# Attention passes of the hybrid block: two branches of a head run as one step instead of one pass per step

## The reference, cut to what matters

```python
s = einsum("bqgrd,bqgkd->bqgrk", q, k) * scale + bias      # selected keys, then once more for the window
p = masked_softmax(s, dist >= 0)
o = einsum("bqgrk,bqgkd->bqgrd", p, v)
o = g[:, :, 0] * o_cmp + g[:, :, 1] * o_slc + g[:, :, 2] * o_win
y = sigmoid(g_conv) * conv_module(...) + sigmoid(g_attn) * nsa_attention(...)
```

## Time and profile before

| | |
|---|---|
| median of 3 runs | 1822.02 us (1819.73 to 1822.78) |
| profiled execution | 1821.97 us, span of its core 1820.2 us |
| PE busy | 1733.0 us, 95% of the span |
| DVE busy | 1250.7 us, 69% |
| ACT busy | 877.8 us, 48% |
| mean granted clock of PE | 0.995 |

### The profile page before, as it was taken

The page is one execution under the profiler, slowest core; times in us unless marked ns, Lnnn a source line. Parts: engine busy times, 40 slices in busy tenths (PEclk is TensorE's granted clock), DMA queues, the critical chain, the costliest instruction groups (busy, mean ns, idle before and its releaser), DMA issues.

```text
span 1820.2 us, 33142 instructions
## 1 busy us (share of the span) xinstructions
PE 1733.0 (95%) x12198; PEld 1588.6 (87%) x12198; DVE 1250.7 (69%) x2120; ACT 877.8 (48%) x1411; POOL 74.3 (4%) x119
## 2 busy tenths in 40 slices
PE   6999999999999999999999999999999999999998
PEld 5899988888999889998778999899877789879997
DVE  6887878568777877766556555589798565555554
ACT  2444457534444434445565444545355655554443
POOL 2000011200000100000000000100000000000000
PEclk9999999999999999999999999999999999999999
DMA  9888847657988688864433655354532154435551
GB/s 352 304 304 295 285 143 201 142 197 245 303 296 289 193 314 291 290 203 133 134 93 92 229 187 184 118 174 147 161 93 76 47 185 163 138 118 196 184 186 67
DMA packets 123657, 352.78 MB, mean 194 GB/s; under 512 B 9850, under 2 KB 52874, under 8 KB 114224
## 3 DMA queue, kind: packets, MB, share of 16 engines
q1 hardware_dynamic: 108128, 262.18, 44.5%
q10 hardware_dynamic: 12432, 78.65, 12.6%
q0 software_dynamic: 3008, 10.74, 1.7%
HBM read 347.31 MB, written 4.22 MB: 193 GB/s over the span
## 4 chain that ended last, share of the span: by engine, by line
PE 72%; DVE 15%; ACT 6%; issue 4%; DMA 2%; POOL 1%; ACTq 0%; DVEq 0%; POOLq 0%
PE ps L779 65%; DVE w_lo L189 3%; DVE arena L2669 2%; ACT w_hi L183 2%; PE ps L354 1%; DVE arena L344 1%; DMA resid<-in_x 1%; DVE resid L1205 1%; DMA arena<-in_mod_w 1%; PE ps L647 1%; DVE act_s L2989 1%; PE ps L3058 1%; PE ps L2976 0%; DVE act_s L3023 0%; DVE tmp L1202 0%
## 5 line engine op out<-in xcount | busy, mean ns | idle before, releaser
L779 PE MATMUL ps<-t_hi,w_hi 128*128 128x256 f32 (+1 forms) x2616 | 748.4, 286 | 12.5 <-DVE t_lo L708 5.4
L779 PE MATMUL ps<-t_lo,w_hi 128*128 128x256 f32 (+1 forms) x2616 | 740.8, 283 | 0.0
L779 PE MATMUL ps<-t_hi,w_lo 128*128 128x256 f32 (+1 forms) x2616 | 740.6, 283 | 0.0
L779 PEld LDWEIGHTS ps<-t_hi,w_hi 128*128 128x128 f32 (+1 forms) x2616 | 500.2, 191 | 28.5 <-issue 14.5
L779 PEld LDWEIGHTS ps<-t_lo,w_hi 128*128 128x128 f32 (+1 forms) x2616 | 500.5, 191 | 2.1
L779 PEld LDWEIGHTS ps<-t_hi,w_lo 128*128 128x128 f32 (+1 forms) x2616 | 500.4, 191 | 0.2
L1066 DVE TENSOR_TENSOR w_lo<-raw,w_hi 128x1024 fp32r<-128x1024 f32 x258 | 313.8, 1224 | 157.2 <-ACT w_hi L1055 157.1
L189 DVE TENSOR_TENSOR w_lo<-raw,w_hi 128x1024 fp32r<-128x1024 f32 x240 | 288.9, 1223 | 151.7 <-ACT w_hi L183 151.6
L1055 ACT ACTIVATE w_hi<-raw 128x1024 fp32r<-128x1024 f32 x258 | 269.4, 1054 | 174.9 <-PE ps L779 174.5
L183 ACT ACTIVATE w_hi<-raw 128x1024 fp32r<-128x1024 f32 x240 | 248.6, 1053 | 147.4 <-PE ps L779 105.6
L779 PE MATMUL ps<-w_hi,g_hi 128*128 128x512 f32 x440 | 176.2, 400 | 5.9 <-DVE g_lo L1097 5.7
(11 more groups left out here) (349 smaller groups left out, 1670.9 us busy)
## 6 DMA issues: line engine op xcount, KB each, us to landing
raw<-in_stream SPq DMA_DIRECT2D x498, 512.0 KB, 4.3
arena<-in_mod_w ACTq DMA_DIRECT2D x72, 1024.0 KB, 6.9
grow<-gate_scratch POOLq DMA_DIRECT2D x6, 512.0 KB, 8.5
u_scratch<-u_keep ACTq DMA_DIRECT2D x1, 3072.0 KB, 35.1
arena<-u_scratch POOLq DMA_DIRECT2D x8, 256.0 KB, 3.2
small<-in_small POOLq DMA_DIRECT2D x1, 1368.0 KB, 11.0
resid<-in_x POOLq DMA_DIRECT2D x1, 1024.0 KB, 18.7
arena<-in_mem POOLq DMA_DIRECT2D x1, 1024.0 KB, 5.3
```

The source lines that it names most:

```text
L779: last = TE.matmul(out, lhs, rhs, start=start and i == 0, stop=stop and i == 2)
```

## The change

`pass_scores` is cut in two. What remains under that name are PE's scores; the reduces, the exp and POOL's load of the bias are the new `pass_softmax`. The reduces now also wait for the transposes of n - 2 (they overwrite what those read; before, the order ensured this). The loop takes two passes at a time, the two branches of one head. With s even, PE's order is scores of s and s + 1, the step's other work (half a block), transposes of s - 2 and s - 1, the other work of s + 1, values of s - 2 and s - 1. DVE's is scaling of s - 2 and s - 1, `w_lo` if due, reduces of s and s + 1, chores and taps of s, `w_lo` if due, chores and taps of s + 1. ACT's is the two copies of the transposes, the two exps, then the work behind s, the output of a pair of heads if due, and the work behind s + 1. No instruction is added or removed.

```diff
--- before.py
+++ after.py
@@ -2953,7 +2953,7 @@
         biasc_free = biasc[:, :, :, :].rearrange("p q n h -> p q (n h)")
         N_PASS = 2 * HEADS
         in_q = ((0, P), (P, 3 * P))
-        sc_read, exp_done, scaled, turned_n, pt_kept = {}, {}, {}, {}, {}
+        scored, sc_read, exp_done, scaled, turned_n, pt_kept = {}, {}, {}, {}, {}, {}
         pv_done, o_kept = {}, {}
 
         def head_of(n):
@@ -2976,14 +2976,17 @@
                     last = TE.matmul(ps[2 + n % 2][:, lo:hi], qT[b:b + 64, pr, q * P:(q + 1) * P],
                                      kd[br][b:b + 64, h // 4, 0:hi - lo], start=True, stop=True)
                 last.then_inc(T.sem, T.up())
-            at = T.n
+            scored[n] = T.n
+
+        def pass_softmax(n):
+            pr, h, br = head_of(n)
             nm = st[:, 20 + 4 * (n % 2):22 + 4 * (n % 2)]
 
             @block.vector
             def _(dve):
                 if n % 4 == 0:
                     dve.wait_ge(pair_bias[pr % 3], 16 * (pr // 3 + 1))
-                dve.wait_ge(T.sem, at)
+                dve.wait_ge(T.sem, max(scored[n], turned_n.get(n - 2, 0)))
                 for q, (lo, hi) in enumerate(in_q):
                     bias = bias_of[pr % 3][:, h % 2, L - (hi - lo):L]
                     VE.tensor_tensor_reduce(out=act_s[:, n % 2, lo:hi], in0=ps[2 + n % 2][:, lo:hi], in1=bias, scale=-1.0,
@@ -3192,12 +3195,7 @@
                 VE.tensor_tensor(t_lo[:, two, :], cv[:, two, :], t_hi[:, two, :].bitcast(F32), ALU.subtract).then_inc(V.sem, V.up())
             kt_ready[2 * pr] = kt_ready[2 * pr + 1] = (V.n, conv_hi[pr])
 
-        for step in range(N_PASS + 2):
-            n = step - 1
-            if 0 <= n < N_PASS:
-                pass_scale(n)
-            if step < N_PASS:
-                pass_scores(step)
+        def beside_passes(step):
             if step == SUM_AT[0]:
                 assert not pending
                 channel_sums(cv, sum_bank(0), (V.n, fill_free[SUM_AT[0] // 4 - 1]))
@@ -3208,18 +3206,34 @@
             else:
                 fill_half()
             fill_lo()
-            if 0 <= n < N_PASS:
-                pass_turn(n)
-            if step >= 2:
-                pass_values(step - 2)
-                if (step - 2) % 4 == 3:
-                    pass_keep((step - 2) // 4)
+
+        def behind_passes(step):
             fill_keep()
             for work in chores.get(step, ()):
                 work()
             if step < SUM_AT[0]:
                 for _i in range(3 if step % 4 == 3 else 2):
                     next_taps()
+
+        for step in range(0, N_PASS + 2, 2):
+            now = (step, step + 1) if step < N_PASS else ()
+            held = (step - 2, step - 1) if step >= 2 else ()
+            for n in held:
+                pass_scale(n)
+            for n in now:
+                pass_scores(n)
+            beside_passes(step)
+            for n in held:
+                pass_turn(n)
+            for n in now:
+                pass_softmax(n)
+            behind_passes(step)
+            beside_passes(step + 1)
+            for n in held:
+                pass_values(n)
+            if step >= 2 and step % 4 == 0:
+                pass_keep(step // 4 - 1)
+            behind_passes(step + 1)
         fill_lo()
         assert fill_at[0] == 32 and not fill_todo and not lo_todo
         for pr in range(4):
```

## The result

The changed kernel took 1827.57 us (median of 20 runs, 1823.50 to 1830.89) against 1821.99 in the same runs: ratio 1.0029, 95% interval 1.0021 to 1.0037. It is slower, by 0.29% by this ratio and by 5.6 us by the medians. One of the 20 runs of the kernel before took 3372.82 us and does not count in the ratio. The changed kernel's 20 times fall into two groups, 9 up to 1826.15 us and 11 from 1827.07 on, and TensorE's mean granted clock over a run mostly goes with them.

| mean granted clock of the run | changed | before |
|---|---|---|
| 0.997 and more | 7 runs, mean 1824.6 | 22 runs, mean 1819.8 |
| between | 5 runs, mean 1826.7 | 52 runs, mean 1823.1 |
| 0.993 and less | 8 runs, mean 1829.7 | 18 runs, mean 1824.3 |

The account below looks back on a forecast made before the run. Taken as bound by DVE from first reduce to channel sums, then by PE to the last values. 1821.97 + 2.7 (+3.25 stage two, -0.55 earlier sums) + 0.3 switches + 1.0 clock = 1826.0 us, range 1822.0 to 1829.5.

Parts of the forecast that it names:

- Stage one, DVE's: First reduce to channel sums, bound by DVE: new reduce wait costs nothing, hidden by w_lo; sums start earlier, -0.55 us.
- the 0.55 of the earlier sums: End of stage one: channel sums wait for pass 19's scaling, not pass 20's reduce, and start at 1397.15: -0.55 us.
- a new wait in stage one: Rival, first stretch: PE over 0.6 late for second transposes, DVE stalls 0.3 in each of ten pairs, +3: 1829; 10%.
- What PE saves: PE's work per pair of passes: 6.65 us, plus up to 0.10, against 7.18; some 0.5 saved.
- that rival: Second scores of a pair, same 64 rows: scores pay again for each weight load, up to 0.2 x 4: 1826.8; 8%.
- Stage two laid out: Channel sums to last values, place by place: 52.2 us against 48.95 before, +3.25.
- The wait for the mean: Half block of step 21 waits for DVE's mean read, now behind reduces 20 and 21: PE loses 1.45 us.
- The 0.3 for the switches: PE's switches costed at nothing, lying between 0 and 1.4 us: 0.3 us taken.
- the signs: What would show it, among others: w_lo waits for ACT's w_hi four times, at steps 23, 25, 29 and 31.
- The clock: Tail: PE idle 4.1 us before transpose 30, granted clock falls to half, costing between 0 and 1.7 us; 1.0 taken.
- the switches decide: Rival: w_lo's and mean do not hold PE, its work up to values 29 shrinks, faster: 1818.1 us; 4%.
- the waits are shorter: Rival: waits shorter than laid out, copies and exps overlap more, tail as before: 1822.5 us; 8%.

Follow-up runs that it names:

- w_lo moved: Changed kernel with a due w_lo made, from step 21 on, at the next even step behind the two scalings: 1820.71 us, 0.9992 to the kernel before.
- The separate edits: Edits of the changed kernel, each run alone: filler first 1.0032, long filler 1.0019, mean first 1.0024, w_lo behind the scalings 0.9992, to the kernel before.
- the repeat: The changed kernel itself run once more, no edit: 1827.54 us, 1.0030 to the kernel before.
- fillers at two of the places: Changed kernel with thirty filler products before transpose 30 and twenty before the channel sums: 1823.35 us, 1.0003 to the kernel before.
- The long filler: Changed kernel with thirty filler products before transpose 30 in place of ten between transposes 30 and 31: 1826.79 us, 1.0019 to the kernel before.
- the filler at the sums: Changed kernel with keep_busy(bank, 10) before the channel sums alone: 1827.23 us, 1.0027 to the kernel before.
- the mean and the filler: Changed kernel, w_lo moved, plus mean read behind the sums and ten filler products before transpose 30: 1820.96 us, 0.9993; with filler before the sums too, 0.9976.

## Why the prediction was right, and where it was not

Slower was forecast, 1826.0 in a range of 1822.0 to 1829.5; it is 1827.57.

- **Stage one, DVE's:** right at full clock. 74.2 us against 74.8, the 0.55 of the earlier sums measured as 0.6. DVE waits in no pass. The rival "a new wait in stage one" comes true when the clock is low at the start of the passes: 1.3 to 1.8 us once (three profiles), not 0.3 in each pair. Its cause is PE's clock, which I priced only in the tail.
- **What PE saves:** right. Scores in a row 1.50, values 1.44, half block behind transposes 1.43 (with w_lo moved; in the changed kernel itself the chain shows none such without a wait). The row-group rule of the Trainium skill (TensorE: Matmul & The Clock Gate, Part 3) would have the second scores pay again, though the same part also lets a weight load run ahead into a background buffer; two scores on the same rows took 1.50 in every pair, so the measurement decides against that rival. The rule on drains of the Trainium skill (TensorEngine Tiling (Array Packing), Tiling Modes, Key Properties) agrees with 1.43. Behind a wait a half block took 1.62 to 1.66 even so.
- **Stage two laid out:** right, place by place. The wait for the mean was forecast as 1.45 and measured as 1.50; transposes 23 for 19.6, and at 19.8 (1415.16); transposes 29 for 42.2, and at 42.4 (1437.79); transposes 30 for 48.6, and at 48.9 (1444.27); the end without the fall for 52.2, and 53.9 less 1.6 is 52.3. The separate edits took these terms away one by one. The 0.3 for the switches came out as 0.1 (52.3 in place of 52.2). Of the signs, w_lo waited for w_hi three times (5.9 us in all) and not four.
- **The clock:** the place in the tail was right and its size too small, 1.0 (the middle of 0 to 1.7) for a measured 1.6. **This is the term that was mis-sized**, and I took the tail for the only place. Without it the passes cost 2.7 more, for a forecast of 3.0. The idle time before the sums grew from 1.6 to 2.5 us and costs 1.5 to 1.7 when the clock falls there; a fall at the start costs 1.3 to 1.8 through the new wait. They part the two profiles of the changed kernel, 128.1 and 131.0 us in the passes; against before's 123.8 these are +4.3 and +7.2, and the measured +5.6 lies between. At a mean clock of 0.997 and more the whole differs by 4.8, which is the +4.3 of the passes nearly; forecast was +4.0. What is above 4.8 in the median may be the clock's chance: the runs of 0.993 and less were 8 of 20 here, 1 of 7 in the repeat, and 18 of 92 for the kernel before. With fillers at two of the places, +2.1 in the passes is left.
- **Still open:** from 0.997 to 0.992 of 1827 us is some 18 us more at half clock (0.005 x 1827 x 2). Profiles show both places for it. The repeat, at 0.995, has 10 us more in the passes than the first profile (13.6 against 3.5; the clock is listed to 0.001, which is 3.7 us). The long filler and the filler at the sums, at 0.994, have 13.7 more ahead of the passes and get there 4.0 to 4.7 us later, which is about what parts the two groups. No run of 0.992 was profiled, so how its falls are shared out, and whether the change has a part in those outside the passes, isn't known.
- The rivals "the switches decide" and "the waits are shorter" did not happen. Their condition was made by moving w_lo, and then the order gave 1.4 us less than before's stretch, and 3.1 less with the mean and the filler.

## What to carry to other kernels

Grouping two short passes saves the switches (some 0.5 us a pair here, 6.65 for 7.18) but puts the exps and scalings of two passes into the wait behind them instead of one's; on a strict queue anything due in between, here w_hi behind the exps and w_lo ahead of the scalings, adds to that chain, so place it behind what the other engine waits for. When an order is changed, look up every single wait that names a bank or buffer read by another chore: the mean's read cost 1.5 us by its place alone. And filler belongs before the first wait of an idle time, not between two pieces that are due (0.6 us here), and it should be no longer than that idle time (the sums came 0.7 late in the kernel before).

## What was not expected of the hardware

The granted clock fell behind shorter idle times than the tail's: with PE busy 1.25 of 3.40 us (2.5 idle in a row) before the sums in one run, and in the first profile the same wait left it at full. Eight of the profiles have a wait of 2.5 to 3.1 us there without filler, and in four of them the clock fell. The same binary's profiles thus differ by 2.9 us in a stretch of 128. Ahead of the passes the kernels are the same, and still the first reduce comes between 1319.88 and 1326.83: near 1321 in the profiles with 3.4 us at half clock ahead of it, at 1325.25 or later in the three with 17.1. So the medians of variants differed less clearly than their stretches: the mean and the filler, worth 1.8 us in the stretch, did not show in the median beside w_lo alone. To price an edit of 1 or 2 us here, read its own stretch and count the falls. At half clock the sums took 5.2 to 5.4 us in place of 3.7 and not 7.4, since the fall lasted 3.4 us.
